# Inverting 32x32 diagonal blocks on VectorE instead of 16x16, with one doubling level less on TensorE

## The reference

```python
a_mat = jnp.where(tri_strict, beta[..., None] * kk * decay, 0.0)
rhs = jnp.concatenate([v * beta[..., None], k * (beta * jnp.exp(G))[..., None]], axis=-1)
sol = lax.linalg.triangular_solve(a_mat + eye, rhs, left_side=True, lower=True, unit_diagonal=True)
```

## Time and profile before

| | |
|---|---|
| time, median of 3 runs | 884.5 us (882.5, 884.5, 884.59) |
| time of the profiled execution | 882.61 us |
| its span in the trace | 880.9 us |
| TensorE busy | 870.1 us (99%) |
| VectorE busy | 580.3 us (66%) |
| ScalarE busy | 492.1 us (56%) |
| GpSimd busy | 120.6 us (14%) |

### The profile page before, as it was taken

How to read it: one execution, slowest core, us unless ns; L and a number is a source line. 1 busy time by engine, 2 the same in 40 slices (tenths; PEclk the granted TensorE clock), 3 DMA queues, 4 the chain that set the end, 5 groups by cost and what they waited for, 6 DMA issues and landing times.

```text
span 880.9 us, 15699 instructions
## 1 busy us (share of the span) xinstructions
PE 870.1 (99%) x6513; PEld 807.9 (92%) x6513; DVE 580.3 (66%) x836; ACT 492.1 (56%) x753; POOL 120.6 (14%) x133
## 2 busy tenths in 40 slices
PE   8999999999999999999999999999999999999998
PEld 8999999889999988888899998999999899998886
DVE  4567664868888756666768887865567665555542
ACT  5566874566666645566676673444554475554330
POOL 6100001211111100223444110000100012220000
PEclk9999999999999999999999999999999999999999
DMA  7843374865655565536544444642246556656550
GB/s 267 295 160 123 99 237 154 281 213 167 201 195 185 180 226 192 191 128 256 186 131 147 159 146 151 185 163 97 97 163 218 176 166 194 191 196 228 174 185 25
DMA packets 132740, 156.87 MB, mean 178 GB/s; under 512 B 9370, under 2 KB 106045, under 8 KB 132413
## 3 DMA queue, kind: packets, MB, share of 16 engines
q1 hardware_dynamic: 125988, 152.30, 52.2%
q10 hardware_dynamic: 6680, 3.56, 1.3%
HBM read 153.61 MB, written 2.24 MB: 177 GB/s over the span
## 4 chain that ended last, share of the span: by engine, by line
PE 88%; DVE 6%; ACT 3%; issue 1%; POOL 1%; DMA 1%; POOLq 0%; ACTq 0%; SPq 0%
PE ps L2080 74%; PE ps L2111 4%; PE ps L2035 4%; PE ps L2032 3%; DVE wl L839 2%; PE ps L2134 1%; ACT wh L1488 1%; PE ps L2388 1%; DVE gkq L873 1%; PE ps L2358 1%; DVE mt L1308 1%; DMA raw<-in_w_up 1%; ACT sS L1693 0%; DVE gp L1059 0%; PE ps L2362 0%
## 5 line engine op out<-in xcount | busy, mean ns | idle before, releaser
L839 DVE TENSOR_TENSOR wl<-raw,wh 128x1024 fp32r<-128x1024 f32 (+1 forms) x278 | 331.4, 1211 | 189.1 <-ACT wh L1488 188.9
L1488 ACT ACTIVATE wh<-raw 128x1024 fp32r<-128x1024 f32 (+1 forms) x292 | 286.6, 1023 | 113.7 <-PE ps L2080 93.1
L2080 PE MATMUL ps<-xh,wh 128*128 128x256 f32 x1248 | 347.2, 280 | 1.5 <-ACT xh L1542 1.1
L2080 PE MATMUL ps<-xh,wl 128*128 128x256 f32 x1248 | 343.3, 277 | 0.0
L2080 PE MATMUL ps<-xl,wh 128*128 128x256 f32 x1248 | 342.0, 277 | 0.0
L2080 PEld LDWEIGHTS ps<-xh,wh 128*128 128x128 f32 x1248 | 233.6, 188 | 3.5 <-ACT wh L1488 0.8
L2080 PEld LDWEIGHTS ps<-xh,wl 128*128 128x128 f32 x1248 | 233.5, 188 | 0.0
L2080 PEld LDWEIGHTS ps<-xl,wh 128*128 128x128 f32 x1248 | 233.0, 188 | 0.2
L703 POOL TENSOR_TENSOR wl<-raw,wh 128x1024 fp32r<-128x1024 f32 (+1 forms) x14 | 33.8, 2415 | 168.1 <-ACT wh L1488 168.1
L2080 PE MATMUL ps<-wh,f2L 128*128 128x512 f32 x128 | 49.8, 389 | 0.0
L2080 PE MATMUL ps<-wh,f2H 128*128 128x512 f32 x128 | 49.8, 389 | 0.0
(11 more groups left out here) (359 smaller groups left out, 1358.0 us busy)
## 6 DMA issues: line engine op xcount, KB each, us to landing
raw<-in_w_in SPq DMA_DIRECT2D x55, 1024.0 KB, 4.8
raw<-in_w_up SPq DMA_DIRECT2D x38, 1024.0 KB, 5.2
raw<-in_w_down SPq DMA_DIRECT2D x26, 1024.0 KB, 4.9
raw<-in_w_out SPq DMA_DIRECT2D x8, 1024.0 KB, 4.9
raw<-in_w_proj_fox SPq DMA_DIRECT2D x4, 1024.0 KB, 5.0
raw<-in_w_proj_gdn SPq DMA_DIRECT2D x4, 1024.0 KB, 5.1
raw<-in_w_conv_branch SPq DMA_DIRECT2D x4, 512.0 KB, 3.4
raw<-in_w_att_branch SPq DMA_DIRECT2D x4, 512.0 KB, 3.4
```

Source lines behind the costliest of these rows:

```text
L839: e.tensor_tensor(L, R, H.bitcast(F32), ALU.subtract).then_inc(lo.sem)
L1488: e.activation(tile_of(WH, u)[:, k:kc, :], tile_of(RAW, u)[:, k:kc, :], ACT.Copy).then_inc(hi.sem)
L2080: k = e.matmul(o, l, r, start=opens, stop=done and n == ends[c], skip_group_check=True)
```

## The change

The blocks that VectorE inverts are 32x32. There are 64 of them; each lies on two partitions, p and p + 64, which both hold the whole block (`U32`), and the even rows of the inverse on the one, the odd rows on the other (`Y32`). The inversion has 31 steps, spread over 25 ticks. The read of the blocks is two DMAs, and the store of the inverses is two. `LEVELS` loses its first level. `INVERT` stands 2 ticks later, the store and the read of the inverses 31 and 35 ticks, the start of Y 38, the first doubling 32, the solve 19, and `o_turn` 12.

```diff
-LEVELS = (16, 32, 64)
-LAST = 2
+LEVELS = (32, 64)
+LAST = 1
...
-BLOCKS_OUT, BLOCKS_IN, INVERT, INVERSES_OUT, INVERSES_IN, START_Y = 33, 40, 47, 55, 59, 65
+BLOCKS_OUT, BLOCKS_IN, INVERT, INVERSES_OUT, INVERSES_IN, START_Y = 33, 40, 49, 86, 94, 103
...
-    return 75 + 9 * i
-SOLVE = 105
+    return 107 + 9 * i
+SOLVE = 124
...
-        U16 = reg("U16", [P, 16, 16], 48)
-        Y16 = reg("Y16", [P, 16, 16], 49)
-        T16 = reg("T16", [P, 64], 50)
-        Yc = reg("Yc", [P, 16, 16], 51)
+        U32 = reg("U32", [P, 32, 32], 32)
+        Y32 = reg("Y32", [P, 16, 32], 36)
+        T32 = reg("T32", [P, 136], 38)
+        Yc = reg("Yc", [P, 16, 32], 48)
...
-                signals(e.memset(Y16[:], 0.0), b16p)
-                in_turn()
-                signals(e.memset(Y16[:].rearrange("p i j -> p (i j)")[:, 0::17], 1.0), b16p)
+                signals(e.memset(Y32[:], 0.0), b16p)
+                for z, rows in enumerate((LO_, UP_)):
+                    in_turn()
+                    signals(e.memset(Y32[rows].rearrange("p r j -> p (r j)")[:, z::34], 1.0), b16p)
...
-                e.wait_ge(blocks_in, 16)
-                for m in range(15):
-                    n, k = m + 1, 15 - m
+                e.wait_ge(blocks_in, 32)
+                for m in range(31):
+                    c, n, k = m + 1, m // 2 + 1, 31 - m
+                    t = T32[:, 0:n * k].rearrange("p (r j) -> p r j", r=n)
+                    v = Y32[:, 0:n, c:32]
                     if m:
                         e.wait_ge(*b16("s", m - 1))
+                    e.tensor_tensor(t, Y32[:, 0:n, m:c].broadcast_to([P, n, k]), U32[:, m:c, c:32].broadcast_to([P, n, k]), ALU.mult
                                     ).then_inc(b16.sem)
                     e.wait_ge(*b16("m", m))
                     e.tensor_tensor(v, v, t, ALU.subtract).then_inc(b16.sem)
-                    if m % 2:
-                        yield from at.to(INVERT + (m + 1) // 2)
+                    yield from at.to(INVERT + 4 * c // 5)
...
-                unit(U_G2 + i, 5 if i == 1 else None, lambda: side.add(o_turn()))
+                unit(U_G2 + i, 1 if i == 3 else None, lambda: side.add(o_turn()))
...
-                e.dma_start(U16[:], blocks[:].rearrange("a s t -> (a s t)").rearrange("(p x) -> p x", p=P)[:, 0:16 * P].rearrange(
-                    "p (i t) -> p i t", t=P)[:, :, 0:16]).then_inc(blocks_in, 16)
+                diagonal = blocks[:].rearrange("a s t -> (a s t)").rearrange("(g x) -> g x", g=64)[:, 0:32 * P].rearrange(
+                    "g (i t) -> g i t", t=P)[:, :, 0:32]
+                for rows in (LO_, UP_):
+                    e.dma_start(U32[rows], diagonal).then_inc(blocks_in, 16)
                 yield from at.to(INVERSES_OUT)
-                e.wait_ge(*b16("s", 14))
-                e.dma_start(inverses[:], Y16[:].rearrange("p i j -> p (i j)")).then_inc(inverses_out, 16)
+                e.wait_ge(*b16("s", 30))
+                flat_ = inverses[:].rearrange("p x -> (p x)")
+                by_parity = flat_.rearrange("(g r z j) -> z g r j", g=64, r=16, z=2)
+                for z, rows in enumerate((LO_, UP_)):
+                    e.dma_start(by_parity[z], Y32[rows]).then_inc(inverses_out, 16)
                 yield from at.to(INVERSES_IN)
-                e.wait_ge(inverses_out, 16)
-                e.dma_start(Yc[:], inverses[:].rearrange("p x -> (p x)").rearrange("(a s j) -> s a j", s=P, j=16)
-                            ).then_inc(inverses_in, 16)
+                e.wait_ge(inverses_out, 32)
+                e.dma_start(Yc[:], flat_.rearrange("(a s j) -> s a j", s=P, j=32)).then_inc(inverses_in, 16)
```

More of the change, by code:

```diff
@@ L159, in two_blocks @@
         MK3 = fixed("mk3", [P, 384])
-        ML = fixed("ml", [P, 2, P])
-        M16 = fixed("m16", [P, P])
+        ML = fixed("ml", [P, LAST, P])
+        M32 = fixed("m32", [P, P])
         COLS = fixed("cols", [P, 276])
@@ L235, in two_blocks @@
         Tm = reg("Tm", [P, 2, 8, P], 40)
-        U16 = reg("U16", [P, 16, 16], 48)
-        Y16 = reg("Y16", [P, 16, 16], 49)
-        T16 = reg("T16", [P, 64], 50)
-        Yc = reg("Yc", [P, 16, 16], 51)
+        U32 = reg("U32", [P, 32, 32], 32)
+        Y32 = reg("Y32", [P, 16, 32], 36)
+        T32 = reg("T32", [P, 136], 38)
+        Yc = reg("Yc", [P, 16, 32], 48)
         blocks = nc.dram_tensor("blocks", [16, P + 1, P], F32)
-        inverses = nc.dram_tensor("inverses", [P, 256], F32)
+        inverses = nc.dram_tensor("inverses", [P, 512], F32)
         gz = reg("gz", [P, 8, T], 60)
@@ L306, in two_blocks @@
                     "ul0", "ul", "ob0", "ob", "mk0", "mk1", "mk", "ml0",
-                    *(f"ml{i}{k}" for i in range(2) for k in "abc"), "mlh", "m0", "m1", "m2", "pp")
+                    *(f"ml{i}{k}" for i in range(LAST) for k in "abc"), "mlh", "m0", "m1", "m2", "pp")
         nsq = steps("norm_sq", "sq")
@@ L383, in two_blocks @@
             sem(n) for n in ("blocks_out", "blocks_in", "inverses_out", "inverses_in"))
-        b16p = steps("blocks_start", "z", "i")
+        b16p = steps("blocks_start", "z", "even", "odd")
         b16 = steps("blocks_inverse", "m", "s")
@@ L674, in late_constants @@
                 signals(e.tensor_tensor(ML[:, :, 0:64], ML[:, :, 0:64], ML[:, :, 64:128], ALU.add), cst)
[L675 to L678, removed]
+                memset(M32[:], 1.0)
+                v = M32[:].rearrange("p (n j) -> p n j", j=32)
+                select(v, ALU.is_ge, 0.0, 0, [[-32, 4], [0, 32]], 1)
+                select(v, ALU.is_ge, 0.0, 31, [[32, 4], [0, 32]], -1)
                 memset(ppow[:], 0.5)
@@ L1156, in gdn @@
                 yield from at.to(INVERT)
-                e.wait_ge(blocks_in, 16)
-                e.wait_ge(*b16p("i"))
-                for m in range(15):
-                    n, k = m + 1, 15 - m
-                    t = T16[:, 0:n * k].rearrange("p (i j) -> p i j", i=n)
-                    v = Y16[:, 0:n, n:16]
+                e.wait_ge(blocks_in, 32)
+                e.wait_ge(*b16p("odd"))
+                for m in range(31):
+                    c, n, k = m + 1, m // 2 + 1, 31 - m
+                    t = T32[:, 0:n * k].rearrange("p (r j) -> p r j", r=n)
+                    v = Y32[:, 0:n, c:32]
                     if m:
                         e.wait_ge(*b16("s", m - 1))
-                    e.tensor_tensor(t, Y16[:, 0:n, m:n].broadcast_to([P, n, k]), U16[:, m:n, n:16].broadcast_to([P, n, k]), ALU.mult
+                    e.tensor_tensor(t, Y32[:, 0:n, m:c].broadcast_to([P, n, k]), U32[:, m:c, c:32].broadcast_to([P, n, k]), ALU.mult
                                     ).then_inc(b16.sem)
@@ L1175, in gdn @@
                     e.wait_ge(*cst("m2"))
-                    e.tensor_tensor(Yt[:, a, 4 * g:4 * g + 4, :].rearrange("p h (n j) -> p h n j", j=16),
-                                    Yc[:, 8 * a + 4 * g:8 * a + 4 * g + 4, :].unsqueeze(2).broadcast_to([P, 4, 8, 16]),
-                                    mid(M16[:], 4).rearrange("p h (n j) -> p h n j", j=16), ALU.mult).then_inc(ch_start[c].sem)
+                    e.tensor_tensor(Yt[:, a, 4 * g:4 * g + 4, :].rearrange("p h (n j) -> p h n j", j=32),
+                                    Yc[:, 8 * a + 4 * g:8 * a + 4 * g + 4, :].unsqueeze(2).broadcast_to([P, 4, 4, 32]),
+                                    mid(M32[:], 4).rearrange("p h (n j) -> p h n j", j=32), ALU.mult).then_inc(ch_start[c].sem)
             def turned_v(c):
@@ L2431, in solve @@
                 for n in (g, g + 2):
-                    e.wait_ge(*ch_dve[n]("Y2"))
+                    e.wait_ge(*ch_dve[n](f"Y{LAST}"))
                 products(3 + g, (lambda h: Yt[:, 0, h, :], w(0)))
@@ L2529, in tensor @@
             for u in range(U_GZ, U_YG):
-                unit(u, XH, XL, at=5 if u == U_G2 + 1 else None, begins=lambda: side.add(o_turn()))
+                unit(u, XH, XL, at=1 if u == U_G2 + 3 else None, begins=lambda: side.add(o_turn()))
             for i in range(4):
```

## The result

The changed kernel is slower: 894.7 us median of four executions (893.73 to 896.0), against 883.5 (882.03 to 884.59) of the kernel before on the same chip. The ratio is 1.0133, 95% interval 1.0117 to 1.0149. The forecast had the sign and the three places of waiting, but +3.0 us where the chip says +11.2. The profiled execution took 893.73 us, with a span of 892.0, 11.1 more than before.

The account below looks back on a forecast made before the run. TensorE, busy 99%, was taken to bound the kernel. The level's -6.2 and waits of 4.6, 1.1 and 3.5 sum to +3.0 us, from 883.6 to 886.6 us, range 880.5 to 890 for 8 in 10.

Parts of the forecast that it names:

- the three places of waiting: TensorE waits for low parts of units 96 and 97 (4.6 us), at `o_turn`'s first transpose (1.1), in unit 106 (3.5).
- -6.2 us for the level: TensorE saves one doubling level: 5.77 us of transposes and two product steps, with slower ticks behind them 6.2 us.
- the waits for the low parts: Units 96 and 97: VectorE starts the inversion at 557.4, comes late with low parts; TensorE waits 4.6 us, three pieces.
- Unit 106: TensorE waits for the last low part of the delta rule's output, taken at 3.5 us.
- `o_turn`, forecast 1.1: Moved 12 ticks later: scaled output ready 7.2 us after unit 103's end, TensorE there after 6.1; wait 1.1 us.
- The 6.9 us for the read of U: Read of the blocks before the inversion, two DMAs: 1.7 + 2 x 2.6 us, between bounds of 4.7 and 8.9.
- 2.6 us on 2,048 runs: Read of U: a DMA of 2,048 runs took 4.3 us, one of 128 runs 1.7; so some 2.6 us.
- the estimate had been 9.0: Read of U by the Trainium skill's packet rule: 9.0 us, TensorE's low-part wait 6.7; forecast 888.7 us in that case.
- a read of up to some 7.5 us is hidden: Read of `Yc` before the first Y: expected 5.3 us as before, hidden up to 7.5; cost nothing, up to 1.
- A late load: Rival: units 99 and 100 get loads 6 to 9 us later, first rounding some 1 us late; 889, chance 0.03.
- the sum had waits at their listed length: The total: -6.2 + 4.6 + 1.1 + 3.5 = +3.0 us, the waits of TensorE added as they stand.
- my rivals: Cover holds, 877.4 us, 0.13; one place waits, 882 to 884.4, 0.27; slow read, 888.6 to 890, 0.15; late load, 0.03.

Follow-up runs that it names:

- drop_level: Kernel before without its first doubling level, blocks still 16x16 (output not the reference's): 876.0 us against 882.65, ratio 0.9935.
- pool_lows: Changed kernel with the second half's low part of units 94 to 99 given to GpSimd: 900.92 us against 882.74, ratio 1.0203.
- before_pool_lows: Kernel before with the second half's low part of units 94 to 99 given to GpSimd: 891.4 us, ratio 1.011.
- short_inversion: Changed kernel with only the first 15 of 31 inversion steps (inverses incomplete): 888.89 us, ratio 1.0062 against the kernel before.
- values_later: Changed kernel with the turned values placed behind the inversion, 30 ticks later: 889.83 us, ratio 1.0062 against the kernel before.
- other_input: Changed kernel with units 106 to 109 multiplying the normed input, not the delta rule's output: 889.91 us, ratio 1.009 against the kernel before.
- one_wait: Kernel before, TensorE at `o_turn`'s transposes 11 ticks earlier: 888.34 us against 882.58, ratio 1.0056; its twin with 25 unread transposes ahead: 886.06, 1.0035.
- all_earlier: values_later with inverse transfers, start of Y, doublings and solve 4 ticks earlier, `o_turn` 3 earlier: 885.46 us, ratio 1.0013 against the kernel before.
- filled_waits: Changed kernel with unread transposes on TensorE, 24 before its wait for Y and 18 before `o_turn`: 892.59 us, ratio 1.0123 against the kernel before.
- two_queues: all_earlier with the read for the upper half of U issued by SP, not ScalarE: 883.26 us, ratio 1.0003 against the kernel before.

## Why the prediction was right and where it failed

**Right: -6.2 us for the level.** drop_level gives -6.6 by its times and -5.9 in the stretch, and the traces count the instructions that were named. **Right in place and near in size:** the waits for the low parts, forecast 4.6, are 3.6 by their lines, since VectorE starts at 556.25 and not 557.4 and steps run as costed (the longest 0.30 us each). Unit 106, forecast 3.5, is 3.1. Together with `o_turn` 8.8 against 9.2; that the sum is so near is luck in part, since one term is 1.0 too large and one 1.0 too small.

`o_turn`, forecast 1.1, is 2.1, because GpSimd's power took 2.55 us and not the 1.64 of the earlier trace rows. The reason stands in the traces. In all 14 profiled kernels this operation (28 times) takes 2.55 us where a low part on VectorE, which reads two tiles of SBUF, was already running when it began, and 1.64 us everywhere else. It is the exclusion of pool_lows the other way round. In the changed kernel the low part begins 0.17 us ahead of the power:

```profile
650.41 1.22 DVE L840 TENSOR_TENSOR wl<-raw,wh 128x1024 fp32r<-128x1024 f32 x1
650.58 2.55 POOL L777 TENSOR_TENSOR gv__83<-gv__83,npow 128x8 f32<-128x8 f32 x1 [7.14 <-DVE gv__83 L1230]
```

The 6.9 us for the read of U from its issue are near what happened, issued at 549.07, used at 556.25, 7.2, but also by luck. The sum put 2.6 us on 2,048 runs, as the difference between a read beside a load of 1 MB and a store that had none for most of its time. In before_pool_lows the read of `Yc`, 2,048 runs of 64 B with no load under way, took 2.8 us in all. And the second issue is not 0.4 us behind the first but 0.7, and holds ScalarE for 2.70 us. By the rule of the Trainium skill ("DMA: Bandwidth & Descriptors", "Why small descriptors are slow (HBM only)") the estimate had been 9.0; the trace does not agree, with 7.2.

**Failed, first step:** "a read of up to some 7.5 us is hidden. Taken at nothing, up to 1 us." The read of `Yc` took 10.8 and TensorE waited 2.9. I took the 5.3 us of before, where one load of 1 MB was under way, though I had just argued that VectorE would work off its backlog right there, and had a rival ("A late load") in which it touches the loads. I gave it 0.03 and looked at loads being late, not at three of them coming together. short_inversion and values_later, with a small or no backlog, read in 4.7 and 5.0 us. What the runs show is that without the backlog the read is short; that the loads close together are the cause is argued from their number at its issue.

**Failed, second step:** the sum had waits at their listed length and nothing behind them. Missing are 4.7 us at the lower clock in three places, and 2.1 us because a listed wait is shorter than the loss from start to start (9 waits, 11.6 us by lines; 13.3 and 0.4 of restarts by starts). other_input (no slow window at unit 106 once the waits are gone) and the pair of one_wait (16 transposes in 3.07 us behind an idle wait, 1.73 behind a filled one) show it. No wait of TensorE before is over 1.7 us, so the price of a longer one had to be marked as unknown and bounded; the prediction put it at nothing and gave no reason.

By the table above: the three forecast waits are 8.8 and not 9.2, the fourth wait is 2.9, the lines' shortfall 2.1, the clock 4.7, the part ahead -1.1; +3.0 so becomes +11.1 within rounding (3.0 - 0.4 + 2.9 + 2.1 + 4.7 - 1.1 = 11.2). With the clock priced, my rivals would have been dearer too, and the chance of "within 0.3%" smaller.

## What to carry to other kernels

Work that is taken from the bounding engine and given to a helper has to fit the helper's gaps where it lands: here 6.2 us gained on TensorE were given back by 17 us on VectorE put into 17 us that already held other work. Price a wait of TensorE of 2 us or more at one and a half times its length or more, as here at nearly every such wait, or give it something to do meanwhile. Where a backlog ends, look for what it frees all at once: the transfers that it lets go will stand beside the next small read. And when work moves in time, ask which operation of VectorE a small one on GpSimd will now meet.

## What the runs showed of the hardware that was not expected

- TensorE's granted clock stayed at 1.00 behind single waits of 1.1 to 1.7 us (all_earlier, the changed kernel at 572). It fell to 0.50 behind waits of 2.1, 2.7 and 2.9 us, behind one of 1.84 (filled_waits), behind 1.2 and 1.1 us close together (two_queues), and behind four pieces of 3.1 us in all within 5 us; 16 transposes then take 3.1 to 3.5 us and not 1.75. It stayed at 1.00 behind a wait of 2.08 us in pool_lows, so the length of a wait alone does not decide. Transposes of the identity in the wait kept it at 1.00.
- Products of 256 columns come every 0.113 or every 0.118 us at the same granted clock of 1.00 (444 against 427 instructions in 50 us).
- The same read, 256 KB in runs of 128 B: 4.7 to 6.9 us with at most one load of 1 MB under way when it was issued, and 10.8 to 11.2 with two.
- A run of 128 B cost no more than one of 64 B: `Yc` with 2,048 runs took 5.3 us before, and 4.7 to 5.5 in four of the five kernels after that also had one load under way (6.9 in the fifth).
- Of two reads of 2,048 runs one behind the other on ScalarE's queue the first held the engine for 0.68 us, the second for 2.70; on two queues each took 0.7.
- GpSimd's subtraction of 2.4 us stops a two-input operation of VectorE for its whole length, and a two-input operation of VectorE that is already running makes GpSimd's power take 2.55 us and not 1.64.
